# Expert passes of at most 128 token columns without the second tile of token rows

## The reference

```python
logits = (xt @ w_router + b_router).astype(jnp.float32)
top_logit, top_e = lax.top_k(logits, TOP_K)          # 4 of 32 experts for each token
gates = jax.nn.softmax(top_logit, axis=-1)
...
hgu = xb @ w_gate_up[e] + b_gate_up[e]               # 1024 -> 2 x 1024
gate, up = jnp.split(hgu, 2, axis=-1)
gate = jnp.minimum(gate, SWIGLU_LIMIT)
up = jnp.clip(up, -SWIGLU_LIMIT, SWIGLU_LIMIT)
act = (up + 1.0) * gate * jax.nn.sigmoid(SWIGLU_ALPHA * gate)
return act @ w_down[e] + b_down[e]                   # 1024 -> 1024
...
y = jnp.zeros((T, D), y_sorted.dtype).at[tok_sorted].add(
    y_sorted * gate_sorted[:, None].astype(y_sorted.dtype))
```

## Time and profile before

| what | value |
|---|---|
| timed runs | 2884.02 us median (2883.94, 2884.02, 2894.53) |
| the profiled execution | 2894.67 us; its span from first to last instruction is 2892.9 us |
| expert stage in the span | about 1061 to 2732 us |
| TensorE busy over the whole span | 2727.8 us, 94% |
| VectorE, ScalarE, GpSimd busy | 37%, 21%, 8% |
| mean granted TensorE clock | 0.948 of 2.4 GHz |
| moved by DMA | 526.65 MB, mean 182 GB/s |

### The profile page before, as it was taken

The page is one execution under the profiler, slowest core; times in us unless marked ns, Lnnn a source line. Parts: engine busy times, 40 slices in busy tenths (PEclk is TensorE's granted clock), DMA queues, the critical chain, the costliest instruction groups (busy, mean ns, idle before and its releaser), DMA issues. The chain is left out here.

```text
span 2892.9 us, 47141 instructions
## 1 busy us (share of the span) xinstructions
PE 2727.8 (94%) x18543; PEld 2337.5 (81%) x18544; DVE 1056.3 (37%) x1908; ACT 613.3 (21%) x1272; POOL 242.8 (8%) x214
## 2 busy tenths in 40 slices
PE   7999998786998979999999999999999999999788
PEld 3345543754985559999999999999999999999666
DVE  2143542946242243222223323232323333333365
ACT  2111222325521111111111111111111111111245
POOL 0000001403620000000000000000000000000130
PEclk9999998658999969999999999999999999999889
DMA  3001010000006226677778888899999999999542
GB/s 132 29 30 58 0 62 33 1 22 1 1 19 215 88 84 196 213 234 236 253 257 267 278 265 286 290 296 292 298 295 304 299 309 296 307 298 302 200 158 75
DMA packets 442841, 526.65 MB, mean 182 GB/s; under 512 B 13716, under 2 KB 408808, under 8 KB 442728
## 3 DMA queue, kind: packets, MB, share of 16 engines
q1 hardware_dynamic: 429448, 478.03, 50.4%
q0 software_dynamic: 13280, 46.93, 5.2%
HBM read 486.39 MB, written 38.54 MB: 181 GB/s over the span
## 5 line engine op out<-in xcount | busy, mean ns | idle before, releaser
L1527 PE MATMUL ex_psum<-ex_xT,weight_ring_a 128*128 128x134 f32 (+14 forms) x6144 | 768.9, 286 | 0.8 <-ACT ex_xT L1513 0.8
L1527 PEld LDWEIGHTS ex_psum<-ex_xT,weight_ring_a 128*128 128x128 f32 x6144 | 759.1, 191 | 1.2 <-issue 1.2
L1567 PE MATMUL ex_psum<-ex_hT,weight_ring_b 128*128 128x134 f32 (+14 forms) x4096 | 521.5, 286 | 0.0
L1567 PEld LDWEIGHTS ex_psum<-ex_hT,weight_ring_b 128*128 128x128 f32 x4096 | 508.1, 191 | 0.0
L1537 DVE TENSOR_SCALAR ex_gate<-ex_psum,bias_gate_up 128x192 f32<-128x192 f32 x256 | 95.0, 413 | 696.6 <-PE ex_psum L1527 681.4
L1527 PE MATMUL ex_psum<-ex_xT,weight_ring_b 128*128 128x134 f32 (+14 forms) x2048 | 255.6, 286 | 0.0
L1527 PEld LDWEIGHTS ex_psum<-ex_xT,weight_ring_b 128*128 128x128 f32 x2048 | 252.2, 191 | 0.0
L1541 DVE TENSOR_SCALAR ex_up<-ex_psum,bias_gate_up 128x192 f32<-128x192 f32 x256 | 95.0, 413 | 401.1 <-PE ex_psum L1527 401.1
L239 PE MATMUL project_psum<-nT,w_in_chunks 128*128 128x512 f32 x512 | 225.2, 603 | 3.4 <-DVE nT L358 3.4
L1554 ACT ACTIVATE ex_sig<-ex_gate 128x384 f32<-128x384 f32 x128 | 67.1, 525 | 718.4 <-DVE ex_gate L1537 711.6
L1575 ACT ACTIVATE ex_yT<-ex_psum,bias_down 128x192 f32<-128x192 f32 x256 | 93.8, 418 | 533.0 <-PE ex_psum L1567 533.0
(11 more groups left out here) (313 smaller groups left out, 2908.6 us busy)
## 6 DMA issues: line engine op xcount, KB each, us to landing
weight_ring_a<-in_w_gate_up SPq DMA_DIRECT2D x192, 1024.0 KB, 6.1
weight_ring_b<-in_w_down SPq DMA_DIRECT2D x128, 1024.0 KB, 6.4
weight_ring_b<-in_w_gate_up SPq DMA_DIRECT2D x64, 1024.0 KB, 5.1
y_dram<-ex_y_a SPq DMA_DIRECT2D x33, 512.0 KB, 3.5
w_in_chunks<-in_w_in SPq DMA_DIRECT2D x7, 2048.0 KB, 8.1
y_dram<-ex_y_b SPq DMA_DIRECT2D x33, 256.0 KB, 3.8
project_work<-in_x SPq DMA_DIRECT2D x8, 512.0 KB, 3.7
gates_dram<-project_work POOLq DMA_DIRECT2D x16, 256.0 KB, 2.3
```

The costliest lines, as they stand in the source:

```text
L1527: mm = pe.matmul(self.ps[:, bank, i * CAP:i * CAP + width], w[:, k, i * P:(i + 1) * P], self.xT[:, k, 0:width], start=(k == 0), stop=(k == ...
L1567: mm = pe.matmul(self.ps[:, bank, i * CAP:i * CAP + width], w[:, k, i * P:(i + 1) * P], self.hT[:, k, 0:width], start=(k == 0 and i == 0), ...
```

## The change

Passes whose rank has at most 128 columns are called narrow; `NARROW` is the number of ranks above that, 19. For a narrow rank the second tile of token rows is not listed, gathered, turned, copied or stored. Since semaphore counts stay as they were, the last increment of a shortened group counts for those left out. The loops of all five queues are split where narrow passes begin. As the rows 128 to 191 of the narrow regions are no longer written, they are filled once from a zeroed `y_b`, with a DMA at the head of SyncE's queue.

```diff
+NARROW = sum(ranks for columns, ranks in PASSES if columns > P)
...
-    def gather(self, pool, x, fill):
+    def gather(self, pool, x, fill, narrow=False):
         pool.wait_ge(self.listed, 2 * x + 2)
         pool.wait_ge(self.turned, fill).then_inc(self.rows_free, 1)
+        if narrow:
+            pool.indirect_dma_start(out=self.rows_a[:], out_offset=None, in_=self.g.xn_dram,
+                                    in_offset=bass.IndirectOffsetOnAxis(ap=self.list_a[:, 0:1], axis=0)).then_inc(self.rows_in[0], 16)
+            return
...
-        for width, lo, at in ((P, 0, 0), (CAP - P, P, 2)):
+        for width, lo, at in ((P, 0, 0),) if narrow else ((P, 0, 0), (CAP - P, P, 2)):
...
+        if narrow:
+            with self.nc.allow_low_precision(reason="token numbers, summed in float32"):
+                dve.tensor_reduce(self.list_a[:, 0:1], self.ps[:, self.LIST, 0:2], AX.X, ALU.add).then_inc(self.listed, 2)
+            return
...
-            pe.transpose(into[:, i * CAP:i * CAP + P], self.rows_a[:, k * P:(k + 1) * P], self.ident)
-            mm = pe.transpose(self.turned_x_pair(q)[:, i * CAP + P:i * CAP + 2 * P], self.rows_b[:, k * P:(k + 1) * P], self.ident)
+            mm = pe.transpose(into[:, i * CAP:i * CAP + P], self.rows_a[:, k * P:(k + 1) * P], self.ident)
+            if not narrow:
+                mm = pe.transpose(self.turned_x_pair(q)[:, i * CAP + P:i * CAP + 2 * P], self.rows_b[:, k * P:(k + 1) * P], self.ident)
         mm.then_inc(self.turned, 1)
...
-    def pe_turn_y(self, pe, fill, kept, q):
+    def pe_turn_y(self, pe, fill, kept, q, narrow=False):
+        if narrow and q >= 2:
+            return
...
-        mm.then_inc(self.turned, 1)
+        mm.then_inc(self.turned, 3 if narrow and q == 1 else 1)
...
+    def store(self, sp, fill, dst_a, dst_b, narrow=False):
         sp.wait_ge(self.turn_kept, fill + 4)
         sp.dma_start(dst_a, self.y_a[:]).then_inc(self.y_out[0], 16)
+        if narrow:
+            sp.wait_ge(self.turn_kept, fill + 4).then_inc(self.y_out[1], 16)
+            return
...
             for i in range(8, 12):
                 load(sp, 0, i)
+            sp.wait_ge(x.y_b_zero, 1)
+            unused = g.y_dram[(NARROW + 1) * CAP:Y_FIRST, :].rearrange("(r n) d -> n r d", n=CAP)[P:CAP]
+            sp.dma_start(unused, x.y_b[:].unsqueeze(1).to_broadcast([CAP - P, E - NARROW, D])).then_inc(x.y_out[1], 16)
             sp.wait_ge(x.order_ready, 1)
...
-            with pool.Fori(0, E) as e:
+            with pool.Fori(0, NARROW - 1) as e:
                 x.gather(pool, e + 1, 8 * e + 4)
+            with pool.Fori(NARROW - 1, E) as e:
+                x.gather(pool, e + 1, 8 * e + 4, narrow=True)
...
+            def passes(first, end, columns):
+                cuts = sorted({first, end} | {c for c in (NARROW - 1, NARROW + 1) if first < c < end})
+                for lo, hi in zip(cuts, cuts[1:]):
+                    if hi == lo + 1:
+                        one_pass(lo, columns, lo + 1 >= NARROW, lo - 1 >= NARROW)
+                    else:
+                        with pe.Fori(lo, hi) as e:
+                            one_pass(e, columns, lo + 1 >= NARROW, lo - 1 >= NARROW)
...
-            dve.memset(x.y_b[:, 0:1], 0.0).then_inc(x.y_out[1], 16)
+            dve.memset(x.y_b[:], 0.0).then_inc(x.y_b_zero, 1)
```

More of the change, by code:

```diff
@@ L1495, in turned_x_pair, with pe_turn_x @@
         return self.ps[:, first[0], first[1]:first[1] + CAP + 2 * P]
-    def pe_turn_x(self, pe, x, fill, q):
+    def pe_turn_x(self, pe, x, fill, q, narrow=False, skipped=0):
         if q == 0:
-            for r in self.rows_in:
-                pe.wait_ge(r, 16 * x + 16)
+            pe.wait_ge(self.rows_in[0], 16 * x + 16)
+            if not narrow:
+                pe.wait_ge(self.rows_in[1], 16 * x + 16 - 16 * skipped)
         pe.wait_ge(self.turn_kept, fill + (q if q < 3 else 2))
@@ L1505, in pe_turn_x, with act_keep_x @@
             k = 2 * q + i
-            pe.transpose(into[:, i * CAP:i * CAP + P], self.rows_a[:, k * P:(k + 1) * P], self.ident)
-            mm = pe.transpose(self.turned_x_pair(q)[:, i * CAP + P:i * CAP + 2 * P], self.rows_b[:, k * P:(k + 1) * P], self.ident)
+            mm = pe.transpose(into[:, i * CAP:i * CAP + P], self.rows_a[:, k * P:(k + 1) * P], self.ident)
+            if not narrow:
+                mm = pe.transpose(self.turned_x_pair(q)[:, i * CAP + P:i * CAP + 2 * P], self.rows_b[:, k * P:(k + 1) * P], self.ident)
         mm.then_inc(self.turned, 1)
-    def act_keep_x(self, act, x, fill, q, after):
+    def act_keep_x(self, act, x, fill, q, after, width=CAP):
         act.wait_ge(self.turned, fill + q + 1)
         act.wait_ge(self.gu_done, after)
-        act.copy(self.xT[:, 2 * q:2 * q + 2, :], self.turned_x(q).rearrange("p (i c) -> p i c", i=2)).then_inc(self.turn_kept, 1)
+        act.copy(self.xT[:, 2 * q:2 * q + 2, 0:width], self.turned_x(q).rearrange("p (i c) -> p i c", i=2)[:, :, 0:width]).then_inc(self.turn_kept, 1)
     def pe_gate_up(self, pe, m, fill_x, c, width):
@@ L1589, in pe_turn_y, with dve_keep_y @@
             mm = pe.transpose(self.ps[0:n, self.TURN, i * P:(i + 1) * P], self.yT[:, 4 * (q % 2) + i, tokens], self.ident)
-        mm.then_inc(self.turned, 1)
-    def dve_keep_y(self, dve, y, fill, q):
+        mm.then_inc(self.turned, 3 if narrow and q == 1 else 1)
+    def dve_keep_y(self, dve, y, fill, q, narrow=False):
+        if narrow and q >= 2:
+            return
         dve.wait_ge(self.turned, fill + q + 1)
@@ L1595, in dve_keep_y @@
         dve.wait_ge(self.y_out[q // 2], 16 * y + 16)
-        dve.tensor_copy(to[0:n, (q % 2) * HALF:(q % 2 + 1) * HALF], self.ps[0:n, self.TURN, :]).then_inc(self.turn_kept, 1)
-    def store(self, sp, fill, dst_a, dst_b):
+        dve.tensor_copy(to[0:n, (q % 2) * HALF:(q % 2 + 1) * HALF], self.ps[0:n, self.TURN, :]).then_inc(self.turn_kept, 3 if narrow and q == 1 else 1)
+    def store(self, sp, fill, dst_a, dst_b, narrow=False):
         sp.wait_ge(self.turn_kept, fill + 4)
         sp.dma_start(dst_a, self.y_a[:]).then_inc(self.y_out[0], 16)
+        if narrow:
+            sp.wait_ge(self.turn_kept, fill + 4).then_inc(self.y_out[1], 16)
+            return
         sp.dma_start(dst_b, self.y_b[:]).then_inc(self.y_out[1], 16)
@@ L1649, in _ @@
                 load(sp, 0, i)
+            sp.wait_ge(x.y_b_zero, 1)
+            unused = g.y_dram[(NARROW + 1) * CAP:Y_FIRST, :].rearrange("(r n) d -> n r d", n=CAP)[P:CAP]
+            sp.dma_start(unused, x.y_b[:].unsqueeze(1).to_broadcast([CAP - P, E - NARROW, D])).then_inc(x.y_out[1], 16)
             sp.wait_ge(x.order_ready, 1)
[L1651 to L1660, removed]
+            for first, end in ((0, NARROW + 1), (NARROW + 1, E - 1)):
+                with sp.Fori(first, end) as e:
+                    following = x.expert_at(sp, e + 1)
+                    for i in range(12):
+                        if i < 8:
+                            sp.wait_ge(x.gu_done, 8 * e + i + 1)
+                        else:
+                            sp.wait_ge(x.dn_done, 4 * e + i - 7)
+                        load(sp, following, i)
+                        if i == 7:
+                            x.store(sp, 8 * e + 4, *rows(e), narrow=first > NARROW)
             def load_embedding():
@@ L1675, in _ @@
             for y in range(E - 1, E + 1):
-                x.store(sp, 8 * y + 4, *rows(y))
+                x.store(sp, 8 * y + 4, *rows(y), narrow=True)
             def body(n, r, e):
@@ L1729, in one_pass @@
                     for q in turns:
-                        x.pe_turn_x(pe, e + 1, 8 * e + 8, q)
+                        x.pe_turn_x(pe, e + 1, 8 * e + 8, q, narrow_x)
+            def passes(first, end, columns):
[3 more added lines that the diff above has]
+                        one_pass(lo, columns, lo + 1 >= NARROW, lo - 1 >= NARROW)
+                    else:
+                        with pe.Fori(lo, hi) as e:
+                            one_pass(e, columns, lo + 1 >= NARROW, lo - 1 >= NARROW)
             first = 0
             for columns, ranks in PASSES:
[L1734 to L1738, removed]
+                passes(first, first + ranks, columns)
                 first += ranks
             for q in range(4):
-                x.pe_turn_y(pe, 8 * E + 4, 8 * E + 4, q)
+                x.pe_turn_y(pe, 8 * E + 4, 8 * E + 4, q, narrow=True)
             def body(n, r, e):
@@ L1746, in body @@
                 for q in range(4):
-                    x.pe_turn_x(pe, n + E + 1, fill, q)
+                    x.pe_turn_x(pe, n + E + 1, fill, q, skipped=E + 1 - NARROW)
                 for c in range(4):
@@ L1762, in _ @@
             act.wait_ge(x.order_ready, 1)
[L1763 to L1770, removed]
+            for first, end in ((0, NARROW - 1), (NARROW - 1, E)):
+                with act.Fori(first, end) as e:
+                    expert = x.expert_at(act, e)
+                    for c in range(4):
```

(18 more changed lines are left out.)

24 lines of the change are left out of this document (12 added, 12 removed).

## The result

| | before | changed |
|---|---|---|
| timed runs, median | 2887.22 us (4 runs, 2883.94 to 2894.53) | 2854.53 us (4 runs, 2846.89 to 2862.29) |
| ratio | | 0.9883, 95% interval 0.9846 to 0.9921 |
| profiled execution | 2894.67 us | 2846.89 us |
| expert stage in the profile, from the memset of rows_b to the next stage's first DMA | 1670.09 us | 1638.23 us |

The forecast was 2853.8 us, 30.2 us less than the median shown then. The medians are now 32.7 us apart, and the expert stages of the two profiled executions differ by 31.9 us. That the median after lies only 0.7 us from the forecast is in part luck: with a fourth run the median before moved up by 3.2 us, and single executions of either kernel lie up to 15 us apart. The gain, and best the gain of the expert stage, is what the forecast can be judged by.

The account below looks back on a forecast made before the run. The prediction took TensorE's instruction count times spacing to bound the late passes. Terms of 27.7 + 4.3 - 0.85 - 0.3 - 0.6 = 30.2 us, off the median 2884.02, gave 2853.8 us, range 2847 to 2867.

Parts of the forecast that it names:

- TensorE's count bounds the passes: In late passes time is TensorE's instructions times their spacing; removed lists and turns save 27.7 us together.
- Transposes at their spacing: Turns of x and y priced at 0.44 us per four transposes: 12.3 us for x, 10.6 us for y.
- The list: 8 of 16 small TensorE matmuls go in each narrow list: 0.34 us, 14 times, 4.8 us saved.
- The hT wait: First down product waits for hT's last chunk, margin 0.04 us left: 0.05 us in 12 passes, 0.6 us lost.
- The tail: Behind the last pass, two quarters of y go and the store lands earlier: 4.3 us saved.
- The memset at the start: VectorE's memset of y_b grows from one column to 64x1024, ahead of the first turn: 0.85 us lost.
- The fill: 3.4 MB on SyncE's queue at 406 GB/s takes 8.4 us, ending near 1086; sharing costs the gather 0.3 us.
- the hole: Stretch from 1078 to 1084 us with DMA at 0.00, before SyncE's next load, into which the fill fits.
- the rival I gave 5 in 100: At the start the first gather waits for the fill: 8.1 us more, gain 22, time 2862 us, chance 0.05.
- The cover of the fill: Expert 1's first loads, even 14 us late behind the fill, have more than 46.95 us until their use.
- Loop borders: 7 new borders of split loops cost nothing; as a rival they stall for instructions, time 2899 us, chance 0.02.
- The sum: All terms, from late passes, tail, start and hT wait, together: 30.2 us gained, about 1.05% less.

Follow-up runs that it names:

- run 1: The changed kernel with y's turn, copy and store as before, no fill, and y_b's small memset: expert stage 1652.55 us, late passes 45.62 to 45.74 us.
- runs 2 and 3: An extra 384-column VectorE memset in the chain to hT's last chunk, in the kernel before (expert stage 1670.90 us) and in the changed kernel (1642.33 us).
- run 3: The changed kernel with an extra 384-column VectorE memset in the chain to hT's last chunk, every pass: late passes 45.12 us, expert stage 1642.33 us.
- run 6: The changed kernel with the fill read from 128 partitions of y_a in place of 64 of y_b: fill at 407 GB/s, expert stage 1638.16 us.
- run 4: The changed kernel with the fill put ahead of expert 0's four w_down loads on SyncE's queue: expert stage 1645.31 us.
- runs 7 and 8: The changed kernel with the fill done three and five times, each waited for by SyncE: expert stage 1639.30 us and 1678.06 us.
- run 9: The changed kernel again, unedited: expert stage 1638.34 us, median 2848.03 us of six runs.

## Why the prediction came true, point by point

- **TensorE's count bounds the passes.** Right. The 14 lists and turns of x and 12 turns of y gave 26.48 + 2.08 = 28.56 us for the 27.7 - 0.6 = 27.1 expected, and no idle time came out.
- **Transposes at their spacing.** Right: 0.22 us a quarter of x and 0.84 to 0.88 us a pass for y (run 1). The 81 ns of the Trainium skill's TensorE page, set against it in the prediction, would have given some 6 us less; the trace decides for 0.105 to 0.11 us.
- **The list.** Mis-sized: I took 16 equal matmuls, 0.34 us for eight. The eight for columns 128 to 191, with 64-column weights, were worth 0.43. Over 14 lists that is 1.2 us more gain.
- **The hT wait.** The place and the margin were right and are shown by runs 2 and 3, the price was not: with 0.04 us left and a hand-over of 0.12 us read in the tail I charged 0.05 us a pass, the mean of 0 and 0.08. The hand-over to a waiting load is 0.05 us (run 3: ready at 2580.27, load at 2580.32), and the remaining margin covers just that. 0.6 us expected, nothing paid.
- **The tail.** 4.3 expected, 4.33 measured from the second copy on.
- **The memset at the start.** 0.85 expected, 0.88 measured up to the first turn.
- **The fill.** Two steps failed, and both stayed without effect here by the order of the queue, not by the argument. The 0.3 us that I put down for the gather came out as nothing (6.7 us to landing, 6.8 before). I took its rate from the loads, 406 GB/s, and it ran at 205 to 211: 64 partitions give half the rate (run 6). It was to end near 1086 in the old time and ended at the hole's very end. And I said that the gather shares with the fill; it waits for most of it and lands at its end (run 4). In the change's order the gather had its turn between the loads of 1 MB, ahead of the fill. Put first, the fill costs 7.1 us, which is the rival I gave 5 in 100, at nearly its price of 8.1.
- **The cover of the fill.** I had named the loads of expert 1 as those who wait. It is y_b's first copy, with some 7 us to spare (runs 7 and 8).
- **Loop borders.** The 17 distances ahead of the first narrow step are the same in both kernels, and TensorE shows no more than 0.1 us of idle time behind it, up to the last pass.
- **The sum.** 30.2 expected, 31.9 measured in the stage: 1.2 more from the list, 0.6 not paid to the hT wait, 0.2 less at the start than the 1.15 expected, and some 0.3 us less from the transposes.
- **The rest.** The 10 us of spread between the runs lie ahead of the expert stage, as left open in the prediction; run 9 names the stretch.

## What to carry to other kernels

Where one engine has no idle time, instructions taken from it are worth their spacing in its queue, not their duration, and instructions of another shape have another spacing. Taking work away also takes cover away: look for the wait that the removed instructions hid, and how much is left of its margin. Do not put one long DMA ahead of a small one on which the next work waits, even on another queue; cut it up, and read a tile's rate from rows of the same number of partitions.

## What the runs showed of the hardware that I had not expected

- A write to DRAM from 64 partitions ran at 201 to 211 GB/s with DMA at a busy share of 0.96 to 0.99; the same bytes from 128 partitions ran at 407 with 1.05. The busy share alone does not show it.
- A gather issued while one DMA of 3.4 MB was running on another queue moved nothing for at least six microseconds, then moved beside its last part and landed together with it, 13.7 us behind its issue. With the same bytes in 13 DMAs it landed in 7.4.
- Eight bf16 matmuls with two moving columns and 128-column weights took 0.29 us; the eight with 64-column weights behind them added 0.43 us.
- The granted clock of one stretch was 0.57 or 0.69 in different executions of the same stages, and the next stage began 7 to 18 us later where it was the lower.
